# The second layer's weighted values from split operands: f32 products replaced by three fp32r products each

## What is computed

```python
a_val, a_gate, z_a, q, k, v, o, z_b, gates = split_cols(h @ w_in, EVEN_SIZES)
h_fwd = mlstm_chunkwise(qh, kh, vh, i_f, f_f)
h_bwd = fl(mlstm_chunkwise(fl(qh), fl(kh), fl(vh), fl(i_b), fl(f_b)))
# C_t = f_t C_{t-1} + i_t v_t k_t^T, n_t = f_t n_{t-1} + i_t k_t,
# h_t = C_t q_t / max(|n_t.q_t|, 1)
hm = rms_norm_2((h_fwd + h_bwd).transpose(0, 2, 1, 3), hn_g.reshape(H_B, DV_B))
```

## Time and profile before

| | |
|---|---|
| median of 3 runs | 815.56 us (815.35 to 815.61) |
| the profiled execution | 815.5 us |
| its span | 813.8 us |
| TensorE busy | 803.3 us, 99% |
| VectorE busy | 506.5 us, 62% |
| ScalarE busy | 475.7 us, 58% |
| granted TensorE clock | full speed in all 40 slices of the page |
| DMA | 143.48 MB, mean 176 GB/s |

### The profile page before, as it was taken

How to read it: one execution, slowest core, us unless ns; L and a number is a source line. 1 busy time by engine, 2 the same in 40 slices (tenths; PEclk the granted TensorE clock), 3 DMA queues, 4 the chain that set the end, 5 groups by cost and what they waited for, 6 DMA issues and landing times.

```text
span 813.8 us, 11531 instructions
## 1 busy us (share of the span) xinstructions
PE 803.3 (99%) x4434; PEld 693.0 (85%) x4434; DVE 506.5 (62%) x759; ACT 475.7 (58%) x754; POOL 44.0 (5%) x74
## 2 busy tenths in 40 slices
PE   8999999999999999999999999999999999999997
PEld 7887888888899999888788788788888898898985
DVE  5757754557567666644455677956675567658553
ACT  6557667564465555534555777339764578566642
POOL 2000000000000000710100112000000010000000
PEclk9999999999999999999999999999999999999999
DMA  7773553745456655786657557435474656276121
GB/s 265 243 237 94 155 163 100 255 166 195 127 190 206 203 181 181 191 238 206 205 172 246 161 165 231 169 106 179 145 245 154 190 167 216 90 211 208 41 86 71
DMA packets 84998, 143.48 MB, mean 176 GB/s; under 512 B 9617, under 2 KB 23174, under 8 KB 84816
## 3 DMA queue, kind: packets, MB, share of 16 engines
q1 hardware_dynamic: 80720, 134.37, 52.5%
q0 software_dynamic: 4160, 8.36, 3.8%
q10 hardware_dynamic: 64, 0.02, 0.0%
HBM read 139.51 MB, written 1.07 MB: 173 GB/s over the span
## 4 chain that ended last, share of the span: by engine, by line
PE 87%; DVE 1%; ACT 1%; issue 0%; DVEq 0%; ACTq 0%
PE acc L1747 20%; PE acc L1749 20%; PE acc L1748 20%; PE acc L1800 5%; PE acc L1802 5%; PE acc L1803 5%; PE aux L1836 2%; PE aux L2112 1%; PE aux L2228 1%; PE aux L1984 1%; PE aux L2057 1%; PE acc L1778 1%; PE acc L1777 1%; PE acc L1774 1%; PE aux L2178 0%; PE aux L2217 0%
## 5 line engine op out<-in xcount | busy, mean ns | idle before, releaser
L422 DVE TENSOR_TENSOR wlo<-raw,whi 128x1024 fp32r<-128x1024 f32 (+4 forms) x258 | 303.1, 1199 | 181.0 <-ACT whi L604 179.4
L604 ACT ACTIVATE whi<-raw 128x1024 fp32r<-128x1024 f32 (+4 forms) x258 | 263.4, 1041 | 198.9 <-PE acc L1749 126.0
L1747 PE MATMUL acc<-whi,a_hi 128*128 128x512 f32 (+4 forms) x560 | 212.7, 380 | 1.0 <-issue 0.4
L1749 PE MATMUL acc<-whi,a_lo 128*128 128x512 f32 (+4 forms) x560 | 209.6, 374 | 0.0
L1748 PE MATMUL acc<-wlo,a_hi 128*128 128x512 f32 (+4 forms) x560 | 209.4, 374 | 0.0
L1747 PEld LDWEIGHTS acc<-whi,a_hi 128*128 128x128 f32 x560 | 105.4, 188 | 21.8 <-issue 3.5
L1749 PEld LDWEIGHTS acc<-whi,a_lo 128*128 128x128 f32 x560 | 105.3, 188 | 18.4
L1748 PEld LDWEIGHTS acc<-wlo,a_hi 128*128 128x128 f32 x560 | 105.4, 188 | 17.4
L1800 PE MATMUL acc<-a_hi,whi 128*128 128x256 f32 x320 | 91.4, 285 | 0.6 <-DVE wlo L422 0.6
L1803 PE MATMUL acc<-a_hi,wlo 128*128 128x256 f32 x320 | 90.7, 283 | 0.0
L1802 PE MATMUL acc<-a_lo,whi 128*128 128x256 f32 x320 | 90.7, 283 | 0.0
(11 more groups left out here) (378 smaller groups left out, 884.3 us busy)
## 6 DMA issues: line engine op xcount, KB each, us to landing
raw<-in_even_w_in SPq DMA_DIRECT2D x54, 512.0 KB, 4.4
raw<-in_w_in SPq DMA_DIRECT2D x49, 512.0 KB, 4.3
raw<-in_w_up SPq DMA_DIRECT2D x32, 512.0 KB, 4.4
raw<-in_w_down SPq DMA_DIRECT2D x32, 512.0 KB, 4.4
raw<-in_even_w_out SPq DMA_DIRECT2D x16, 512.0 KB, 4.4
raw<-in_odd_w_in SPq DMA_DIRECT2D x16, 512.0 KB, 4.8
raw<-in_odd_w_out SPq DMA_DIRECT2D x12, 512.0 KB, 4.4
raw<-in_w_branch_gla SPq DMA_DIRECT2D x8, 512.0 KB, 3.5
```

Of the source, the lines that this page charges most:

```text
L422: return e.tensor_tensor(w_view(wlo[u % SPLIT], u), w_view(raw[u % RAW], u), w_view(whi[u % SPLIT], u).bitcast(F32), ALU.subtract)
L604: act.activation(w_view(whi[u % SPLIT], u), w_view(raw[u % RAW], u), ACT.Copy).then_inc(sem("hi_done"), 1)
L1747: pe.matmul(acc_of(c, t), ah[:, ts], hi[:, k], start=first, stop=False)
L1749: ins = pe.matmul(acc_of(c, t), al[:, ts], hi[:, k], start=False, stop=last)
```

## The change

Both operands of the weighted values are split in two parts, and each f32 product becomes three products of fp32r operands: scores hi x values hi, scores hi x values lo, scores lo x values hi. The columns with the ones take part in two of them, which are 258 columns wide; the one in the middle is 256 wide.

- ScalarE: the copies of ev0 and ev1 now round to fp32r (`values_hi`) and no longer free the accumulators. New is `scores_hi(h)`, 128x768 elements: heads 0 and 1 between `pump("ev1")` and `values_hi(1)`, heads 2 and 3 behind `numerators(0)` and `numerators(1)`.
- VectorE: `values_lo(0)` (two instructions of 128x512) behind `pump("ev0", 3)`, `values_lo(1)` behind `pump("ev1")`; these free the accumulators. `scores_lo(h)` (128x768): heads 0 and 1 inside the loop that scales `DW`, behind head 1 and head 2; heads 2 and 3 behind `denominators(0)` and `denominators(1)`. It waits for `scores_hi(h)`.
- TensorE: `numerators(h)` waits for `scores_lo(h)` instead of the scaling, and has 18 products for 6.
- The split scores have two buffers for two heads each, laid over `EQT` and over `FT`, `AVM` and part of `FI`; `EVL` lies over `WS`. Nothing else is moved in memory.

```diff
+            DWH = sb("DWH", [P, 2, 2, 384], F32R, c=c3q)
-            EV = sb("EV", [P, NT, 4, 258], c=c3)
+            EV = sb("EV", [P, NT, 4, 258], F32R, c=c3e)
+            EVL = sb("EVL", [P, NT, 4, TOK], F32R, c=c3s)
+            DWL = sb("DWL", [P, 2, 2, 384], F32R, c=c3f)
...
+                def values_hi(n):
+                    for t in range(NT):
+                        acc_wait(act, f"ev{n}", t)
+                        act.activation(EV[:, t, 2 * n:2 * n + 2, 0:256], acc_of(f"ev{n}", t).rearrange("p (h v) -> p h v", h=2),
+                                       ACT.Copy, scale=rms(2, t)).then_inc(sem("ev_hi"), 1)
+
+                def scores_hi(h):
+                    aux_done(act, ("kq", h))
+                    if h >= 2:
+                        aux_wait(act, ("num", h - 2, 1, 1))
+                    act.activation(flat(DWH[:, h % 2]), flat(DW[:, h]), ACT.Copy).then_inc(sem("dw_hi"), 1)
+
                 pump("ev0")
-                for t in range(NT):
-                    copy_out("ev0", EV[:, t, 0:2, 0:256], t, scale=rms(2, t))
+                values_hi(0)
                 pump("ev1")
-                for t in range(NT):
-                    copy_out("ev1", EV[:, t, 2:4, 0:256], t, scale=rms(2, t))
+                scores_hi(0)
+                scores_hi(1)
+                values_hi(1)
                 group_rstd(1)
                 for h in range(4):
                     numerators(h)
+                    if h < 2:
+                        scores_hi(h + 2)
                     pump("eo0", h + 1)
...
+                def values_lo(n):
+                    for t in range(NT):
+                        dve.wait_ge(sem("ev_hi"), 2 * n + t + 1)
+                        hs = slice(2 * n, 2 * n + 2)
+                        acc_free(dve.scalar_tensor_tensor(out=EVL[:, t, hs], in0=acc_of(f"ev{n}", t).rearrange("p (h v) -> p h v", h=2),
+                                                          scalar=rms(2, t), in1=EV[:, t, hs, 0:256].bitcast(F32),
+                                                          op0=ALU.mult, op1=ALU.subtract), f"ev{n}")
+
+                def scores_lo(h):
+                    dve.wait_ge(sem("dw_hi"), h + 1)
+                    dve.tensor_tensor(flat(DWL[:, h % 2]), flat(DW[:, h]), flat(DWH[:, h % 2]).bitcast(F32), ALU.subtract
+                                      ).then_inc(sem("dw_lo"), 1)
+
                 pump("ev0", 3)
+                values_lo(0)
                 conv_rows(1)
                 group_stats(1)
                 pump("ev1", 2)
...
                     aux_free(ins, key)
+                    if h in (1, 2):
+                        scores_lo(h - 1)
                 pump("ev1")
+                values_lo(1)
...
                 for h in range(4):
                     denominators(h)
+                    if h < 2:
+                        scores_lo(h + 2)
                     pump("eo0", h + 1)
...
-                    aux_done(pe, ("kq", h))
+                    pe.wait_ge(sem("dw_lo"), h + 1)
...
-                                ins = pe.matmul(b[:, 0:257], DW[:, h, d, P * blk:P * blk + P], EV[:, st, h, 0:257],
-                                                start=i == 0, stop=i == len(src) - 1)
+                                hi, lo = (buf[:, h % 2, d, P * blk:P * blk + P] for buf in (DWH, DWL))
+                                pe.matmul(b[:, 0:258], hi, EV[:, st, h, 0:258], start=i == 0, stop=False, skip_group_check=True)
+                                pe.matmul(b[:, 0:256], hi, EVL[:, st, h], start=False, stop=False, skip_group_check=True)
+                                ins = pe.matmul(b[:, 0:258], lo, EV[:, st, h, 0:258], start=False, stop=i == len(src) - 1,
+                                                skip_group_check=True)
```

More of the change, by code:

```diff
@@ L266, in program @@
             EQK = sb("EQK", [P, 2, NT, 512], c=c3)
+            c3q = ExitStack()
+            DWH = sb("DWH", [P, 2, 2, 384], F32R, c=c3q)
+            c3q.close()
             EQT = sb("EQT", [P, 2, 4, TOK], c=c3)
-            EV = sb("EV", [P, NT, 4, 258], c=c3)
+            c3e = ExitStack()
+            EV = sb("EV", [P, NT, 4, 258], F32R, c=c3e)
+            c3e.close()
+            after_ev = sb("after_ev", [P, NT * 4 * 258], c=c3)
             ETMP = sb("ETMP", [P, NT, 512], c=c3)
             gng, gnb = sb("gng", [P, D], c=c3), sb("gnb", [P, D], c=c3)
+            c3s = ExitStack()
+            EVL = sb("EVL", [P, NT, 4, TOK], F32R, c=c3s)
+            c3s.close()
             WS = sb("WS", [P, 2, D], c=c3)
@@ L280, in program @@
             bst, bag = sb("bst", [P, 16, 6], c=c3), sb("bag", [P, 16, 2], c=c3)
+            c3f = ExitStack()
+            DWL = sb("DWL", [P, 2, 2, 384], F32R, c=c3f)
+            c3f.close()
             FT = sb("FT", [P, 3, 2 * P], c=c3)
@@ L291, in program @@
             SZA = flat(EQT[:, :, :, :]).rearrange("p (t n) -> p t n", t=NT)
-            post_g = flat(EV[:, 0])[:, 0:D]
+            post_g = after_ev[:, 0:D]
             YTMP = AV
@@ L1339, in _ @@
                 dve.memset(rone[:, 1], 0.0)
-                chain(dve.memset(EV[:, :, :, 256:257], 1.0))
+                chain(dve.memset(EV[:, :, :, 256:258].bitcast(F32), 1.0))
                 dve.memset(epsc[:, 3:4], 0.0).then_inc(sem("even_consts"), 1)
```

## The result

The changed kernel takes 818.15 us (median of five, 817.74 to 819.02), the kernel before 815.35 in the same comparison (814.97 to 815.61). The ratio is 1.0039, 95% interval 1.0028 to 1.0049: **2.8 us slower**, where 818.6 and about 3 us more were forecast.

What follows compares the result with a forecast made beforehand. TensorE, busy 99% of the span, was taken as the bound. Head 1 starting 4.22 us late, less 1.26 saved over three heads with units, gave +2.96 us: 818.6 us against the median of 815.56, range 817.3 to 820.

Steps and rivals of the forecast that it cites:

- The products: TensorE's four heads: 18 split products take 2.16 us a head, saving 0.46 each, 1.84 in all.
- The rival of dear 258-column products: TensorE's heads: 258 columns cost as f32, 0.218 us each, 3.92 a head; 823.7 us, chance 0.03.
- The values: VectorE before the convolution's rows: `values_lo(0)`, 1.28 us, fits into 1.57 us idle and costs nothing.
- The place of the scores: VectorE waits 4.4 us before `scores_lo(0)` for ScalarE, idle 5.15 us before its weight split; head 1 starts 4.22 us later.
- The waits don't add up: TensorE's waits around head 0 (0.5, 1.6, 2.6 us): the last one decides, so head 1 moves by 4.22 us.
- The two thin waits before heads 2 and 3: TensorE waits 0.07 us before head 2 and 0.08 before head 3 for VectorE's denominators and ScalarE's copy.
- chain to head 1: VectorE's and ScalarE's queue from 529.70 to head 1's start at 539.77: 9.6 us, some twenty instructions.
- The gain alone: VectorE's lateness is absorbed in the heads and only the 1.84 us saving shows: 813.7 us, chance 0.12.
- The clock: TensorE's new waits bring half clock; head 1 and its unit cost up to another 4.9 us: up to 823.4, chance 0.10.

Runs made afterwards that it cites:

- the two runs in the good order: Changed kernel with scores rounded early, four heads scaled first, second values pair late: 813.46 us; the same with six f32 products a head, remainders unused: 815.14 us.
- The run with f32 products: Changed kernel, its splits and order kept, but numerators(h) has six f32 products of the rounded parts, remainders unused: 820.66 us.
- each of the two moves: Changed kernel with ScalarE's first score rounding ahead of its waiting weight split: 814.22 us; or with VectorE's four-head scaling and a weight split before the subtractions: 814.63 us.
- both with the late pair: Changed kernel with early score rounding, VectorE's scaling in one piece first, and `values_lo(1)` behind head 0's denominators: 813.46 us.
- One step beyond: Changed kernel with ScalarE's first two score roundings behind the copies of the second values chunk: 821.13 us.
- the later rounding: Changed kernel with `scores_hi(0)` and `scores_hi(1)` moved behind `values_hi(1)` on ScalarE: 821.13 us, ratio 1.0073.

## Why the prediction was right

- **The products.** Forecast 2.16 us a head by the turned products; measured 2.15 (543.83 to 545.98) with 258 columns in two of three. The rival of dear 258-column products is out: they start every 0.12 us. The forecast saving of 1.84 in all agrees with the two runs in the good order, which are 1.7 us apart.
- **The values.** The first pair was to fit into the idle 1.57 us: it took 1.40 of busy time, and 0.55 of idle time was left behind it. Right.
- **The place of the scores.** VectorE's wait was forecast at 4.4 us and is 4.21; ScalarE's 5.15 us ahead of it came out to the hundredth. Head 1 was to start 9.56 us after the request for head 0 and starts 9.49 after it. Moving ScalarE earlier, VectorE's work forward, or ScalarE later changed the time by -3.9, -3.5 and +3.0 us, where -4.0, -3.6 and +2.3 were expected of them.
- **The waits don't add up.** 0.42, 1.19 and 2.28 us before head 0, inside it and before head 1, as the forecast had them (0.5, 1.6, 2.6) a little shorter; only the start of head 1 counts. The run with f32 products, in which head 0's dearer products left the start of head 1 where it was, shows it.
- **What was off.** The two thin waits before heads 2 and 3 (0.07 and 0.08) don't exist. In the changed kernel bank 0 is free for head 2 at about 543.4 and asked for at 543.83, a margin of 0.43. The term was VectorE's and ScalarE's list per head: 4.68 us in the profile (denominators of head 1 at 541.95, of head 2 at 546.63) where I had summed 4.95. I had added durations where starts count: the rounding starts 0.73 us after the pair of copies that is 0.84 long (538.25 to 538.98), and likewise at other seams. Three small errors partly cancel: 0.15 less for the two waits, 0.07 less for the shorter chain to head 1, and 0.08 more because head 1's own products took 2.24 us and not 2.16 (the first starts after the wait are 0.19 apart and not 0.12). That makes the 2.82 of the profile out of the forecast 2.96.
- **The rivals.** The gain alone (0.12) did not come, but it is real: each of the two moves brings back the loss and part of the gain (1.1 and 0.7 us below the kernel before, the second within the noise), and both with the late pair nearly the whole. The clock (0.10) did not fall in the changed kernel's profile; one of the other four executions had a mean of 0.997, and where its clock fell, if it did, is not shown. One step beyond (0.4 to 2.7 us in the first wait) it fell in the profile, and the mean was 0.997 or less in every execution. The margin to it was small: that the clock stayed up, and the forecast with it, is in part luck.

## What to carry to other kernels

When a cheaper operation needs an extra hand-over between two engines, look up first what the giving engine is standing in front of at that moment, and then what the taking engine has queued behind its new wait. Here 1.7 to 1.9 us could be saved and 4.7 were lost by the places of a few instructions, 3.9 of them by that of one pair in ScalarE's list. Where two engines hand work to each other inside a loop, put all work that needs no hand-over ahead of the wait; either that or an earlier start of the giver gave back most of the loss here, and each can be seen in the timelines before anything is built. Sum a chain of short instructions by their starts, not by their durations.

## What the runs showed of the hardware

In the profile of the later rounding the granted clock fell to its lower level although the longest single wait was 2.71 us: TensorE had been idle 2.71, 1.18 and 2.28 us within 12 us, with products between, and head 1's 18 products took 3.75 us instead of 2.24. With the first wait filled by idle transposes, two of five executions had a mean clock as low, with all three filled none, each of these runs on another chip. With the f32 products and waits of 0.42, 0.86 and 2.21 us four of five were at 0.996. In the profile of the kernel before the clock falls only after the last product.

It differs from execution to execution: the same kernel with one wait filled took 819.73 us in an execution at 0.999 and 823.11 in one at 0.997. Why a given execution falls and another doesn't was not settled.

The Trainium skill, "TensorE: Matmul & The Clock Gate", section "HAM oscillation — how this bites in real kernels", describes short bursts of products between waits for DMA that are longer than the bursts, with the half clock in every burst. These runs agree that waits between products can bring the half clock back. The case is another one, though: the waits are for VectorE and ScalarE, and the products between the second and the third (535.53 to 538.74) last longer than any of them.
